# Main products of 256 columns into one half bank, and VectorE multiplying units out of PSUM

## The reference, cut to what matters

```python
def rms_norm(x, w):
    xf = x.astype(jnp.float32)
    y = xf * lax.rsqrt(jnp.mean(xf * xf, axis=-1, keepdims=True) + NORM_EPS)
    return (y * w.astype(jnp.float32)).astype(x.dtype)
...
    h = rms_norm(x, norm1_w[l])
    proj = h @ w_in[l]
...
    mixed = g_nsa * (o_nsa @ w_up_nsa[l]) + g_dn * (o_dn @ w_up_dn[l])
    x = x + mixed @ w_o[l]
    h2 = rms_norm(x, norm2_w[l])
    x = x + (jax.nn.silu(h2 @ w_ffn_gate[l]) * (h2 @ w_ffn_up[l])) @ w_ffn_down[l]
```

## Time and profile before

| | us |
|---|---|
| median of 3 runs | 2800.72 (2800.12 to 2802.66) |
| time of the profiled execution | 2797.75 |
| its span, first to last instruction | 2795.9 |
| TensorE products busy | 2754.8 |
| TensorE weight loads busy | 2431.0 |
| VectorE busy | 2012.8 |
| ScalarE busy | 1370.3 |
| POOL busy | 484.0 |

### The profile page before, as it was taken

One profiled execution on the slowest core, in us unless ns is written; L12 is line 12 of the kernel. 1 busy time (PEld: TensorE's weight loads), 2 busy tenths in 40 slices (PEclk: granted clock), 3 DMA queues, 4 the chain that ended last, 5 costly groups with the idle time before them and its releaser, 6 DMA issues.

```text
span 2795.9 us, 42233 instructions
## 1 busy us (share of the span) xinstructions
PE 2754.8 (99%) x16660; PEld 2431.0 (87%) x16660; DVE 2012.8 (72%) x3057; ACT 1370.3 (49%) x2059; POOL 484.0 (17%) x526
## 2 busy tenths in 40 slices
PE   8999999999999999999999999999999999999998
PEld 7888888888888888888888888888998888888887
DVE  7987897776766666656657889868677777667655
ACT  6453555455554554444436545533554444444434
POOL 2221111100111111001102633620111111001001
PEclk9999999999999999999999999999999999999999
DMA  6544334455555555555556433321465555555555
GB/s 225 166 158 159 128 130 151 150 188 189 191 188 193 188 191 194 189 191 193 190 181 211 160 106 120 106 76 61 149 199 192 192 189 191 193 189 192 193 179 160
DMA packets 133396, 474.72 MB, mean 170 GB/s; under 512 B 14800, under 2 KB 15056, under 8 KB 132944
## 3 DMA queue, kind: packets, MB, share of 16 engines
q1 hardware_dynamic: 133200, 472.02, 51.4%
HBM read 469.87 MB, written 2.10 MB: 169 GB/s over the span
## 4 chain that ended last, share of the span: by engine, by line
PE 87%; DVE 8%; ACT 2%; POOL 1%; issue 1%; DMA 0%; SPq 0%; DVEq 0%; ACTq 0%; POOLq 0%
PE ps L957 86%; DVE ringl L1942 3%; DVE U L1942 3%; POOL U L2613 1%; DVE U L1951 1%; ACT high L1468 1%; PE ps L960 0%; DVE U L1948 0%; DVE xT L1942 0%; DVE U L2137 0%; DMA xT<-in_x_dram 0%; POOL U L2686 0%; DVE U L2225 0%; DVE hx L1942 0%; DVE U L2146 0%
## 5 line engine op out<-in xcount | busy, mean ns | idle before, releaser
L957 PE MATMUL ps<-hr,high 128*128 128x512 f32 x4672 | 1490.1, 397 | 12.1 <-DVE ringl L1942 11.0
L1942 DVE TENSOR_TENSOR ringl<-ring,high 128x1024 fp32r<-128x1024 f32 x888 | 1086.5, 1226 | 438.2 <-ACT high L1468 437.6
L1468 ACT ACTIVATE high<-ring 128x1024 fp32r<-128x1024 f32 x888 | 915.5, 1033 | 615.8 <-PE ps L957 602.8
L957 PEld LDWEIGHTS ps<-hr,ringl 128*128 128x128 f32 x4672 | 879.3, 188 | 192.4 <-issue 0.7
L957 PE MATMUL ps<-hr,ringl 128*128 128x256 f32 x4672 | 924.0, 279 | 0.0
L957 PEld LDWEIGHTS ps<-hr,high 128*128 128x128 f32 x4672 | 718.4, 188 | 21.1 <-issue 14.8
L957 PE MATMUL ps<-yur,high 128*128 128x512 f32 (+1 forms) x2432 | 681.0, 369 | 2.9 <-issue 1.6
L2613 POOL TENSOR_TENSOR U<-U,rs 128x256 f32<-128x256 f32 x292 | 272.9, 935 | 1651.7 <-DVE U L1942 1632.4
L957 PEld LDWEIGHTS ps<-yur,ringl 128*128 128x128 f32 x2176 | 399.3, 188 | 80.4 <-issue 0.7
L1468 ACT ACTIVATE U<-ps 128x256 f32<-128x256 f32 (+4 forms) x481 | 173.7, 372 | 573.1 <-PE ps L957 556.6
L957 PE MATMUL ps<-yur,ringl 128*128 128x256 f32 x2176 | 429.1, 279 | 0.0
(11 more groups left out here) (179 smaller groups left out, 1239.8 us busy)
## 6 DMA issues: line engine op xcount, KB each, us to landing
ring<-in_w_dram SPq DMA_DIRECT2D x862, 512.0 KB, 3.3
ring<-in_w_dram SPq DMA_DIRECT2D x48, 256.0 KB, 3.4
xT<-in_x_dram SPq DMA_DIRECT2D x3, 512.0 KB, 8.5
out_dram<-hx SPq DMA_DIRECT2D x3, 512.0 KB, 2.7
cst<-in_cst_dram SPq DMA_DIRECT2D x1, 1438.5 KB, 13.0
yT<-in_lora_dram SPq DMA_DIRECT2D x1, 1024.0 KB, 7.8
xT<-in_x_dram SPq DMA_DIRECT2D x2, 256.0 KB, 5.0
U<-in_lora_dram SPq DMA_DIRECT2D x1, 512.0 KB, 5.5
```

The source lines that it names most:

```text
L957: return e.matmul(out, l, r, start=start, stop=stop)
L1468: return e.activation(out, i, ACT.Copy, scale=scale)
L1942: return e.tensor_tensor(out, a, b, op)
```

## The change

All main units that are split into high and low now run the narrow form: three products of 256 columns a k-step, into the first half of the bank. A unit then leaves its bank in one step by VectorE: times `rs` for units of a normed input (287 of the 292), the combination with the gate for `up`, one addition to `xT` for `wo` and `down`. ScalarE's copy, VectorE's addition of the second half, and POOL's product are gone for these. Exempt are `gates`, the first unit of `dn` and the three of `lora` (`scaled_later`): ScalarE copies them and POOL multiplies, with no addition between. What ScalarE waited for ahead of its copy (a buffer to be free) VectorE now waits for ahead of its product, and whoever waited for POOL's `sc` waits for VectorE's `free`. The planner's entries follow, and its `TILE` is 0.341 where it was 0.346.

```diff
-TILE, TILE4, TILE33, ROWS = 0.346, 0.432, 0.23, 0.70
+TILE, TILE4, TILE33, ROWS = 0.341, 0.432, 0.23, 0.70
...
+        def by_vector(u):
+
+            return u.kind not in ("cmpkc", "cmpvc", "vs", "vw", "uv", "uq", "uk") and not scaled_later(u)
+
+        def scaled_later(u):
+            return u.i < index[("dn", 0, 0, 1)] or u.kind == "lora"
...
-            work["DVE"].append((m - 0.5, sum(JOIN if u.kind == "wout" else 2 * JOIN + 0.1 if sums_x(u) or u.kind == "up" else JOIN for u in then) + JOIN * later.count("up"),
-                                [("end" if sums_x(u) else "half", u.i) for u in then], [("free", u.i) for u in then]))
-            work["POOL"].append((m - 0.5, SCALE * len(both_), [("free", u.i) for u in both_], [("data", u.i) for u in both_]))
+                                [("free", u.i) for u in own] + [("data", u.i) for u in own if not scaled_later(u)], "exp" if mixed else None))
+            work["DVE"].append((m - 0.5, JOIN * (len(then) + later.count("up")),
+                                [("end", u.i) for u in then], [("free", u.i) for u in then] + [("data", u.i) for u in then]))
+            work["POOL"].append((m - 0.5, SCALE * len(scaled), [("free", u.i) for u in scaled], [("data", u.i) for u in scaled]))
...
-                            c = mact if one_half(prev) else mdve
+                            c = mdve if by_vector(prev) else mact
...
-                                if u.kind == "wout":
-                                    for n_, half in enumerate(moving(u, k0 + k)):
-                                        mm(out[:, 0:SEQ], wh, half, start and n_ == 0, False)
-                                else:
-                                    mm(shaped(out[:, :], 2, SEQ), wh, halves(u, k0 + k), start, False)
-
+                                for n_, half in enumerate(moving(u, k0 + k)):
+                                    mm(out[:, 0:SEQ], wh, half, start and n_ == 0, False)
...
-            def rest(u, dst):
-
-                e.wait_ge(mact.sem, mact.after("half", u.i))
-                tt(dst, dst, ps[u.bank][:, SEQ:2 * SEQ], ADD).then_inc(mdve.sem, mdve.inc("free", u.i))
-
             def evac0(u):
-                key = u.key
-                if one_half(u):
+                if not by_vector(u):
                     return
+                key, src = u.key, ps[u.bank][:, 0:SEQ]
+                if u.i in FIRSTS:
+                    e.wait_ge(mpe.sem, mpe.after("first", u.i))
+                else:
+                    e.wait_ge(used.sem, used.after(u.end()))
                 if u.kind == "up":
                     part, t = key
                     s = sg[t % 4]
-                    rest(u, um[:, t % 2, :])
                     e.wait_ge(mact.sem, mact.after("sig", 16 * part + t))
-                    e.wait_ge(mdve.sem, mdve.last())
                     if part == 0:
-                        stt(mixT[:, t, :], s, 1.0, um[:, t % 2, :], ADD, MUL).then_inc(mdve.sem, mdve.inc("sg", t))
+                        stt(mixT[:, t, :], s, 1.0, src, ADD, MUL).then_inc(mdve.sem, mdve.inc("free", u.i))
+                        mdve.also("sg", t)
...
+                    elif u.kind == "rw":
+                        q, j = key
+                        if q >= 2 * STREAMS:
+                            e.wait_ge(rpe[q % STREAMS].sem, rpe[q % STREAMS].after("rows", q - 2 * STREAMS))
...
+                    tt(place_of(u), src, rs, MUL).then_inc(mdve.sem, mdve.inc("free", u.i))
+                    return
+                x = xT[:, key[-1], :]
+                if u.kind == "wout" and key[0] == 0:
+                    e.wait_ge(ldve.sem, ldve.after("xs", key[1]))
+                if u.kind == "wo":
+                    i = stt(x, src, 0.5, x, MUL, ADD)
                 else:
-                    rest(u, place_of(u))
+                    i = tt(x, x, src, ADD)
+                i.then_inc(mdve.sem, mdve.inc("free", u.i))
...
             def evac0(u):
                 tag = summed_in(u)
-                if normed(u):
-                    e.wait_ge(mdve.sem, mdve.after("free", u.i))
+                if scaled_later(u):
+                    e.wait_ge(mact.sem, mact.after("free", u.i))
```

More of the change, by code:

```diff
@@ L669, in build @@
         sg += [ar.take(SEQ), ar.take(SEQ)]
-        um = ar.take(2, SEQ)
         assert ar.at <= dn0
@@ L847, in build @@
             ends = p.ends.get(m - 1, [])
-            own = [u for u in ends if not sums_x(u)]
-            both_ = [u for u in ends if not one_half(u)]
+            own = [u for u in ends if not by_vector(u)]
+            then = [u for u in ends if by_vector(u)]
+            scaled = [u for u in ends if scaled_later(u)]
             later = [u.kind for u in p.ends.get(m - 2, [])]
@@ L1512, in evac0 @@
                 src, key = ps[u.bank][:, 0:SEQ], u.key
-                if u.kind in ("down", "wout", "wo"):
+                if by_vector(u):
                     if summed_in(u) and (u.kind == "wout" or key[-1] == 15):
@@ L1995, in evac0 @@
                         mdve.also("sg", 16 + t)
-                elif u.kind in ("wo", "down", "wout"):
-                    x = xT[:, key[-1], :]
-                    if u.i in FIRSTS:
-                        e.wait_ge(mpe.sem, mpe.after("first", u.i))
-                    else:
-                        e.wait_ge(used.sem, used.after(u.end()))
-                    if u.kind == "wout" and key[0] == 0:
-                        e.wait_ge(ldve.sem, ldve.after("xs", key[1]))
-                    parts = 1 if u.kind == "wout" else 2
-                    for j in range(parts):
-                        src = ps[u.bank][:, SEQ * j:SEQ * j + SEQ]
-                        if u.kind == "wo":
-                            i = stt(x, src, 0.5, x, MUL, ADD)
-                        else:
-                            i = tt(x, x, src, ADD)
-                        i.then_inc(mdve.sem, mdve.inc("free", u.i) if j == parts - 1 else mdve.inc())
-                        if j < parts - 1:
-                            e.wait_ge(mdve.sem, mdve.last())
-                    if summed_in(u) not in ("", "final_g") and key[-1] == 15:
-                        low_of(summed_in(u), 15)
-                else:
-                    rest(u, place_of(u))
@@ new lines, in evac0 @@
+                x = xT[:, key[-1], :]
[3 more added lines that the diff above has]
+                    i = stt(x, src, 0.5, x, MUL, ADD)
+                else:
+                    i = tt(x, x, src, ADD)
+                i.then_inc(mdve.sem, mdve.inc("free", u.i))
+                if summed_in(u) not in ("", "final_g") and key[-1] == 15:
+                    low_of(summed_in(u), 15)
```

121 lines of the change are left out of this document (53 added, 68 removed).

## The result

The change made the kernel slower. The median is 2842.22 us (2840.93 to 2842.54, 4 runs) against 2801.69 us for the kernel before in the same comparison (2800.12 to 2804.99, 4 runs): a ratio of 1.0142, with a 95% interval of 1.0125 to 1.016. The forecast was 2767 us, with a range up to 2795: it has the wrong sign, and the time lies 47 us above its range. Rival A, the slow pace everywhere, had named 2855. The profiled execution took 2842.54 us, 44.8 us more than that of before (2797.75), with a span of 2840.8 us.

What follows compares the result with a forecast made beforehand. TensorE's product stream was taken as the bound. Terms of -33.0 (k-steps), -1.3 (`up`), -0.4 (end) and +1.3 (full VectorE slices) gave -33.4 us from 2797.75, so 2764.3; with 2.97 for the median, 2767 us, range 2758 to 2795.

Steps and rivals of the forecast that it cites:

- Rival A: All main units: the third weight load leaves the stream no slack, 353.3 ns a k-step, 2855 us in total; chance 0.09.
- I take 340.0, because the 94 pairs have the block layout: 6592 k-steps go from 345.0 ns to the 340.0 seen in 94 pairs of `wout`, 33.0 us gained.
- The slow samples: `vs` at 353.3 ns a k-step and `wout` in 256-column blocks at 355, put down as short and among side products.
- The argument from waits on borders: The 94 pairs of `wout` cross many block borders and semaphore waits, which supported taking 340.0 ns a k-step.
- `up` was misread: The 256 k-steps of `up`, read as 350 ns each, would gain a further 1.3 us at 340.0.
- Rival C: `hr` and `down` units: the 5 ns come from where inputs lie, so only the end is gained, 2800 us; chance 0.06.
- The rule of 2.5 ns a product: Main products each cost a fixed 2.5 ns extra, 16.5 us in all, ending near 2817; chance 0.04, shared with another rival.
- the exit costs nothing on the path: Emptying banks in one VectorE step is off TensorE's path, since three banks take turns; costed at nothing.
- VectorE's product 421 ns for 418: VectorE's product of PSUM and SBUF was foreseen at 418 ns against 417 for the addition it replaces.
- 0.46 us gained at the end for 0.4: After the last product VectorE makes one addition instead of two, 0.4 us gained on the path.
- VectorE at 48.1 us of 50 in its full slices: Where VectorE is nearly full, TensorE would wait for its side chains; 1.3 us lost, bounds 0 and 8.8.
- no moved wait: VectorE's new buffer waits could delay `ringl`, which TensorE needs; three blocks in stock, 8.2 us of work, would hide it.

Runs made afterwards that it cites:

- `apart48`: The changed kernel with its inputs 48 instead of 16 floats past the weight rings' alignment; median 2776.93 us, ratio 0.9939.
- `probe1`: No layers, only 104 bare streams of main products at several distances between inputs and weights; at 16 floats 0.680 or 0.707 us a pair.
- `kick_ffn`: The changed kernel with 31 products split in two, in every fourth `gate` unit and the first of each `down`, `wo`, `wout` group; 2791.46 us, ratio 0.9963.
- `kick_more`: The changed kernel with one product split in every `hr` unit but `fup`, 147 splits; 2799.65 us, ratio 0.999.
- `probe2`: No layers, bare streams with other splits, product orders and distances; with a 128 + 128 split at distance 16, 4 of 6 streams were fast.
- `form_alone`: The kernel before with the narrow form in all main units and its old exit, VectorE's addition replaced by a stand-in; 2839.61 us, ratio 1.013.
- `apart48_kick`: The changed kernel with inputs 48 floats past the rings' alignment and the 31 split products of `kick_ffn`; 2778.74 us, ratio 0.9911.
- `apart48_kick_side`: `apart48_kick` with 75 more split products, in units of `dn`, `q`, `lora`, `rw` and `lat`; 2782.83 us, ratio 0.993.
- `probe3`: No layers, bare streams with varied input columns and weight tile widths; 0.670 us a pair for 128 to 224 columns at the full granted clock.

## Why the prediction was wrong

**The step that failed** is "I take 340.0, because the 94 pairs have the block layout". It counted 94 pairs as 94 samples. They are one: a stream that is left alone keeps its pace, here for 6332 products in a row. What looked like the safest row of the trace was a single sample, and the same code came out the other way in the kernel after. The sample isn't drawn anew in each execution: the four of the kernel after lie within 1.6 us, and only `apart48` shows two groups of times some 28 us apart. The term was given as -33.0 us; on the slow pace it is 6592 x 8.3 ns = +54.7.

**The slow samples were rated wrongly.** The 353.3 ns of `vs` and 355 of `wout` in blocks of 256 columns were put down as short and among side products. `vs` was the slow pace, and so was one of the two pairs of `wout` (0.707). The other had its high inputs at a distance of 32 floats and took 0.713, as pairs do there in `probe1` (0.708 to 0.715). `probe1` shows the slow pace with nothing else at work and side products without effect, and `probe1` also shows that tiles 256 apart are not what makes it.

**The argument from waits on borders doesn't hold.** That the 94 pairs crossed block borders without a slow one showed that borders don't turn the pace. It was read as showing that the slow pace doesn't occur. What turns a stream is elsewhere: the side products of the norm did it five times out of five at distance 16, and they were in neither row of the prediction.

**`up` was misread.** Only the 128 k-steps of its second part were slower in the kernel before, 0.700 or 0.706 a pair; those of the first part ran at 0.690, though their inputs lie as far apart. The second part is the one whose high inputs are at 0 modulo 64. In the kernel after it took 0.703 a pair (351.5 ns a k-step), and the first part, where nothing disturbed it, the slow 353.3, where 340.0 had been assumed.

**Rival A had the mechanism's place and size nearly right.** Its decision point of 115.0 ns a product parts the two paces, 113.3 and 117.8. Its price of 8.3 ns a k-step is what the trace shows (353.3 - 345.0). Its 2855 was 13 us too high, for it put all stretches on the slow pace and the exit at nothing. The starts of the stages in the two traces give the account:

| stage | start before, us | start after, us | longer by, us |
|---|---|---|---|
| start to second part of `mg` | 0 | 0 | 10.2 |
| `mg` and `up`, second part, and `wo` | 575.4 | 585.6 | -2.3 |
| first FFN | 797.3 | 805.2 | 14.7 |
| layer two to the end of `wout` | 1529.5 | 1552.1 | 5.2 |
| second FFN | 2053.4 | 2081.2 | 17.6 |
| after the last main product | 2782.8 | 2828.2 | -0.5 |

That is the 44.9 us between the two spans (the medians are 40.5 apart). The second FFN is its 2112 k-steps x 8.3 ns; the first took 2.8 us more than the second in the kernel before. Fast `mg` and `wo` gave a little back. In its mechanism (the third load leaves the stream no slack) rival A is neither shown nor refuted. Its chance of 0.09 was the fault.

**Rival C, placement,** was right that the place of the inputs matters, and wrong in how: not high and low side by side, but the distance of inputs from weights modulo 64 floats. It moves a pair between 0.680 and 0.720. What C took from `up` as evidence was most likely this too.

**The rule of 2.5 ns a product** had the sign of the result and not its cause. By the fast pace six products cost less than the four of the wide form (0.680 against 0.690), as said in the prediction; the change lost because of a state of the stream that the rule doesn't know. The rule was also used where it isn't meant: the Trainium skill, page "TensorE: Matmul & The Clock Gate", section "Back-to-back issue gap", gives the 2.5 ns for a product by itself, and says that in a stream of loads and products both set the distance. The trace agrees that the 2.5 ns don't give the stream's pace: 113.3 or 117.8 ns for 256 columns. Another rule bears on this. Of the reads the Trainium skill, page "TensorE: Matmul & The Clock Gate", section "Step-by-step: what each phase is for", says that TensorE has two independent read ports, so that loading the next weights takes no read bandwidth from the running product. No run here shows the ports; but the pace changes with the distance of the two operands (0.680 at 48, 0.707 at 16, 0.720 at 0), which is hard to explain if the two reads never meet. The same page, section "LDWEIGHTS (loading the stationary operand)", gives a load as its columns over 1.2 GHz, which is 106.7 ns for 128 as an estimate; the runs show no load by itself, and 111.7 ns for load and product at 128 to 224 columns.

**What held:** the exit costs nothing on the path (it gives 3.6 us); VectorE's product 421 ns for 418; 0.46 us gained at the end for 0.4; ScalarE's copies and 287 of POOL's products gone; VectorE at 48.1 us of 50 in its full slices doesn't hold TensorE; no moved wait shows up as a delay of `ringl` (9.3 us of waits for it, 11.0 before). Waits for `xT` at the start of units grew from 1.0 to 6.0 us, but all of TensorE's waits add up to 31 us in both kernels.

**What stays open:** what in the chip keeps the two paces apart. That the reads of weights and inputs collide is inferred from the distances. Nor is it settled why a stream enters one pace or the other, why a single split turned slow streams in the FFNs of `kick_ffn` (4 of 4), seldom in `kick_more` (21 of 56) and not in `probe2` (0 of 3), and what in the four side products turns a fast one. No kernel with those products moved or left out was run.

## What to carry to other kernels

A pace read from one long stretch is one sample if the stretch was entered once: look for the same form in several stretches, and look at what stands in the stream where a pace changes. When one row of the trace is slower without a reason that you can name, price the change by that row too. When weight loads are recorded as busy for the whole of a stretch, the stream has no slack that you can see, and where the operands lie in SBUF becomes a parameter: here one constant was worth 65 us of 2842. Sweep such a constant with a small probe of the bare stream before judging a form, and look at every execution's time, because a state can show as two groups of times, as in `apart48`.

## What the runs showed of the hardware

- A stream of weight load and product, 256 columns of `fp32r` each time, has two steady paces at a distance of 16 floats modulo 64: 113.3 and 117.8 ns a product, in 2 and in 14 of the 16 streams of `probe1`, and kept for up to 6332 products. At 48 it was 113.3 in 8 of 10 plain streams, at 0 always 120.0.
- Four side products inside such a stream turned it from fast to slow at distance 16, in 5 of 5 cases (kernel after, `form_alone`, `kick_more`, `kick_ffn` twice), and left it fast at 48, in 6 of 6 (`apart48`, `apart48_kick`, `apart48_kick_side`).
- From 128 to 224 columns the pace is 111.7 ns a product at any of three distances at the full granted clock, and 213.3 at a granted clock of 0.50 (128 and 192 columns, `probe3`).
- A product split into two of 128 columns costs 0.11 us (0.13 at distance 48) and can turn the pace: from slow to fast at a single split in 4 of 4 cases in the FFNs of `kick_ffn` but only 21 of 56 in `kick_more`, and in `probe2` in 0 of 3 at a single split and 3 of 3 at the second. It never turned a fast stream slow in `kick_ffn` or `kick_more`, in 61 cases.
- The wide k-steps vary less: 0.690 to 0.702 a pair in the mean of a stream at all distances tried in `probe1`, 0.700 or 0.706 in the second part of `up` in the kernel before. Products of 512 columns with a load each take 226.7 ns at 0, 228.9 at 16 and 233.3 at 48.
